# A block kernel's sixth norm takes the early form, and every head rounds its fourth weight tile ahead of its first evacuation

## What is computed

```python
h = rms_norm(x, gain) * (1.0 + scale) + shift      # the norm ahead of a sublayer
y = h @ w_first                                    # its first projection, in 128-column tiles
...
x = x + (1.0 + gate) * out                         # the residual behind it
```

## Time and profile before

| | |
|---|---|
| median of 3 runs | 3580.46 us (3576.4 to 3591.96) |
| the profiled execution | 3580.06 us, its span 3578.2 us |
| PE busy, share of span | 3448.2 us, 96% |
| DVE, ACT, POOL busy | 2018.7 us (56%), 1212.7 us (34%), 360.7 us (10%) |
| granted PE clock, mean | 0.983 |
| w_hi (L246), w_lo (L252) | 475 and 480 of them, mean 1097 and 1321 ns |

### The profile page before, as it was taken

One profiled execution on the slowest core, in us unless ns is written; L12 is line 12 of the kernel. 1 busy time (PEld: TensorE's weight loads), 2 busy tenths in 40 slices (PEclk: granted clock), 3 DMA queues, 4 the chain that ended last, 5 costly groups with the idle time before them and its releaser, 6 DMA issues. The chain is left out here.

```text
span 3578.2 us, 56582 instructions
## 1 busy us (share of the span) xinstructions
PE 3448.2 (96%) x22456; PEld 2780.9 (78%) x22456; DVE 2018.7 (56%) x2820; ACT 1212.7 (34%) x1783; POOL 360.7 (10%) x264
## 2 busy tenths in 40 slices
PE   7999999999999999999999999999988999999998
PEld 5888777878888788876678888877757787878886
DVE  6666666846665666575443433365666773464343
ACT  3222346432222322243343322233434543233231
POOL 1000003410000000000101000130103330010000
PEclk9999999999999999999999999999979999989999
DMA  6554321125553455421032222222210002223232
GB/s 246 197 193 169 125 76 71 55 93 188 188 207 139 179 191 203 156 86 54 1 112 88 96 97 106 84 88 83 63 33 6 8 6 73 95 65 100 89 99 71
DMA packets 103765, 382.75 MB, mean 107 GB/s; under 512 B 11424, under 2 KB 15136, under 8 KB 103200
## 3 DMA queue, kind: packets, MB, share of 16 engines
q1 hardware_dynamic: 103584, 380.15, 30.7%
HBM read 378.01 MB, written 2.10 MB: 106 GB/s over the span
## 5 line engine op out<-in xcount | busy, mean ns | idle before, releaser
L457 PE MATMUL bank<-h_hi,w_hi 128*128 128x512 f32 x2576 | 1015.5, 394 | 29.2 <-DVE w_lo L252 26.5
L459 PE MATMUL bank<-h_hi,w_lo 128*128 128x512 f32 x2576 | 1005.6, 390 | 0.0
L458 PE MATMUL bank<-h_lo,w_hi 128*128 128x512 f32 x2576 | 1005.3, 390 | 0.0
L252 DVE TENSOR_TENSOR w_lo<-w_raw,w_hi 128x1024 fp32r<-128x1024 f32 (+2 forms) x480 | 634.3, 1321 | 397.7 <-ACT w_hi L246 386.5
L246 ACT ACTIVATE w_hi<-w_raw 128x1024 fp32r<-128x1024 f32 (+2 forms) x475 | 521.1, 1097 | 299.8 <-PE bank L459 260.4
L457 PEld LDWEIGHTS bank<-h_hi,w_hi 128*128 128x128 f32 x2576 | 485.3, 188 | 146.5 <-DVE w_lo L252 30.0
L459 PEld LDWEIGHTS bank<-h_hi,w_lo 128*128 128x128 f32 x2576 | 485.0, 188 | 102.4
L458 PEld LDWEIGHTS bank<-h_lo,w_hi 128*128 128x128 f32 x2576 | 485.5, 188 | 100.7 <-issue 1.9
L457 PE MATMUL bank<-f_gu_hi,w_hi 128*128 128x512 f32 x704 | 278.5, 396 | 0.0
L458 PE MATMUL bank<-f_gu_lo,w_hi 128*128 128x512 f32 x704 | 278.2, 395 | 0.0
L459 PE MATMUL bank<-f_gu_hi,w_lo 128*128 128x512 f32 x704 | 278.2, 395 | 0.0
(11 more groups left out here) (645 smaller groups left out, 4759.4 us busy)
## 6 DMA issues: line engine op xcount, KB each, us to landing
ada_tiles<-in_ada SPq DMA_DIRECT2D x180, 512.0 KB, 4.3
w_raw<-in_gu SPq DMA_DIRECT2D x176, 512.0 KB, 4.4
w_raw<-in_dn SPq DMA_DIRECT2D x64, 704.0 KB, 5.0
w_raw<-in_w_ff SPq DMA_DIRECT2D x64, 512.0 KB, 3.5
w_raw<-in_w_hyb SPq DMA_DIRECT2D x36, 512.0 KB, 3.4
w_raw<-in_w_rkv SPq DMA_DIRECT2D x24, 512.0 KB, 3.5
w_raw<-in_w_attn SPq DMA_DIRECT2D x20, 512.0 KB, 3.5
w_raw<-in_w_hout SPq DMA_DIRECT2D x16, 512.0 KB, 3.4
```

Of the source, the lines that this page charges most:

```text
L252: K.nc.vector.tensor_tensor(K.w_lo[:, half, 0:kb * P], K.w_raw[:, slot, 0:kb * P], K.w_hi[:, half, 0:kb * P].bitcast(F32), ALU.subtract).t ...
L457: nc.tensor.matmul(K.ps[bank][:], wh, hi, start=start, stop=False)
L458: nc.tensor.matmul(K.ps[bank][:], wh, lo, start=False, stop=False)
L459: last_mm = nc.tensor.matmul(K.ps[bank][:], wl, hi, start=False, stop=stop)
```

## The change

1. `hybrid` is given `follow`, the `Modulated` of f01, which is now built with early=True. Its out projection makes the gain at its start and splits x times gain after each residual, on ACT behind the square and on DVE behind the residual. The parts go to `hyb_ahead_hi` and `hyb_ahead_lo`, in the chunks of `proj` from `GATE` and from `Z`. `early_tile` reads them there; in the other heads `ahead_hi` and `ahead_lo` are h_hi and h_lo as before.
2. In every early head the weights of tile 3 are rounded (ACT) and subtracted (DVE) at t == 0, ahead of evacuation 0, instead of at t == 1 behind it. What they wait for is as before.

```diff
@@ gemm, ACT and DVE bodies @@
                     if head and isinstance(i, int) and t < 3:
-                        if t < 2 and not (early and t == 0):
+                        if early and t == 0:
+                            split_hi(K, act, kb, 3 % RING, 1, g0 + 3)
+                        elif t < 2 and not early:
                             split_hi(K, act, kb, (t + 2) % RING, t % SPLIT, g0 + t + 2)
...
                     if head and isinstance(i, int) and t < 3:
-                        if t < 2 and not (early and t == 0):
+                        if early and t == 0:
+                            split_lo(K, dve, kb, 3 % RING, 1, g0 + 3)
+                        elif t < 2 and not early:
                             split_lo(K, dve, kb, (t + 2) % RING, t % SPLIT, g0 + t + 2)
@@ early_tile @@
-                    hi, lo, bank, start, stop = mm(c, 0)
+                    _, _, bank, start, stop = mm(c, 0)
+                    hi, lo = head.ahead_hi[:, c, :], head.ahead_lo[:, c, :]
@@ class Modulated @@
         self.gain, self.scale, self.shift, self.early = gain, scale, shift, early
+        self.ahead_hi, self.ahead_lo = K.h_hi, K.h_lo
...
     def ahead_act(self, act, o):
         K = self.K
-        K.nc.scalar.activation(K.h_hi[:, bass.ds(o, 1), :], K.x[:, bass.ds(o, 1), :], ACT.Identity, scale=K.gain[:, bass.ds(o, 1)]).then_inc(K.h_hi_done.sem, 1)
+        K.nc.scalar.activation(self.ahead_hi[:, bass.ds(o, 1), :], K.x[:, bass.ds(o, 1), :], ACT.Identity, scale=K.gain[:, bass.ds(o, 1)]).then_inc(K.h_hi_done.sem, 1)
...
@@ hybrid @@
-def hybrid(K, nxt, head, gate):
+def hybrid(K, nxt, head, gate, follow):
...
     squares = Squares(K, "hyb", A + 2 * DC * CH)
+    follow.ahead_hi = K.at("hyb_ahead_hi", [P, DC, S], F32R, A + GATE * CH)
+    follow.ahead_lo = K.at("hyb_ahead_lo", [P, DC, S], F32R, A + Z * CH)
...
             act.wait_ge(free.sem, free(o + 1))
+            act.wait_ge(K.x_written.sem, K.x_written(follow.GAIN_STEPS))
             squares.by_act(act, K.x[:, o:o + 1, :], o, o % 2)
+            follow.ahead_act(act, o)
...
             v.scalar_tensor_tensor(x, K.ps[HOUT_BANK[o]][:], K.coef[:, o:o + 1], x, ALU.mult, ALU.add).then_inc(free.sem, 1)
+            follow.ahead_dve(dve, o)
...
         dve.wait_ge(K.coef_done.sem, K.coef_done(1))
+        follow.gain_ahead(dve)
...
+    follow.ahead_advance()
     free.base += DC
@@ build @@
-            elif step != "hyb":
+            else:
                 follow = Modulated(K, *terms(K, *places[plan[n + 1]]), early=True)
...
-                    hybrid(K, nxt, head, gate)
+                    hybrid(K, nxt, head, gate, follow)
```

More of the change, by code:

```diff
@@ L720, in ahead_dve @@
         dve.wait_ge(K.h_hi_done.sem, K.h_hi_done(o + 1))
-        K.nc.vector.scalar_tensor_tensor(K.h_lo[:, bass.ds(o, 1), :], K.x[:, bass.ds(o, 1), :], K.gain[:, bass.ds(o, 1)],
-                                         K.h_hi[:, bass.ds(o, 1), :].bitcast(F32), ALU.mult, ALU.subtract).then_inc(K.h_ready.sem, 1)
+        K.nc.vector.scalar_tensor_tensor(self.ahead_lo[:, bass.ds(o, 1), :], K.x[:, bass.ds(o, 1), :], K.gain[:, bass.ds(o, 1)],
+                                         self.ahead_hi[:, bass.ds(o, 1), :].bitcast(F32), ALU.mult, ALU.subtract).then_inc(K.h_ready.sem, 1)
     def ahead_advance(self):
```

## The result

The changed kernel takes 3602.59 us (median of 8 runs, 3594.4 to 3613.21), the kernel before 3584.1 us (8 runs, 3576.4 to 3593.84). The ratio is 1.0047 with the interval 1.0033 to 1.006: 16.8 us slower (11.8 to 21.5). It is not the quotient of the two medians, which lie 18.5 us apart. The forecast was 15.0 us slower, 3595.1 us when counted from the one execution that the prediction started from (3580.06 us); the kernel before measures 4.0 us more than that here.

The account below looks back on a forecast made before the run. PE was taken to bound the kernel, busy 96% of the span. Terms of -2.25 (early f01 head), +12.0 (DVE queue) and +5.3 (clock) gave +15.0 us, 3595.1 us from 3580.06; recorded range 3577 to 3602 us.

Parts of the forecast that it names:

- Part A: f01's head made early, with its parts made in the hybrid's out projection: 2.25 us gained, throttled stretch included.
- Idle DVE: In hyb, ml, f10, f01 and b2, DVE would stand idle about 1.9 us before tile 3's `w_lo`.
- hyb 1.91, ml 1.94: In these two heads tile 4 would start later by 1.91 us (hyb) and 1.94 us (ml).
- f10 3.08: In f10's head the second modulation transfer is issued later, so tile 4 starts 3.08 us later; bounds 1.3 to 4.1.
- f01 3.08: f01's new early head has the same DVE queue as f10's, so tile 4 again starts 3.08 us later.
- b2 1.98: In b2's head, DVE's delayed queue would cost 1.98 us ahead of tile 4.
- The clock: Long PE idle gaps ahead of tile 4 lower its clock: 1.05 us for each of five heads, 5.3 us in all.
- the one priced gap: The 4.49 us of PE idle before 543.12, whose following tile took 7.71 us against 5.7: a 2.0 us price.
- the second rival: Full clock price after every long gap ahead of tile 4: 10 us of clock, +19.8 us, 3599.8 us; chance 0.20.
- f11 nothing: In f11's head DVE has nothing to do before tile 3, so the reordering would lose nothing.
- gain at tile 3 kept: Rival: tile 4's wait is set by something that doesn't move, so the pull pays: -6.7 us, 3573.4 us; chance 0.14.
- The out projection kept its cover: Rounding ahead costs nothing there, 0.8 us of cover staying; the rival, cover lost, adds 3 us, 3598.1 us; chance 0.04.

Follow-up runs that it names:

- e1: The changed kernel with tile 3's weights put back behind evacuation 0, leaving only f01's early head; 3584.47 us, ratio 0.9988 to the kernel before.
- e2: The kernel before with only tile 3's weights moved ahead of evacuation 0, f01 keeping the old head; 3599.64 us, ratio 1.0033.
- e7: The changed kernel with only DVE's new order, ACT's edit undone; a single run, 3599.22 us.
- e9: The changed kernel with throwaway matmuls between tiles 3 and 4, 20 in f01 and f10, 16 in hyb, ml and b2; 3599.62 us, ratio 1.0037.
- e5: The changed kernel with tile 4's weights also rounded and subtracted ahead of evacuation 2; 3585.27 us, ratio 0.9994 to the kernel before.
- e3: The changed kernel with throwaway matmuls between tiles 3 and 4, 20 in f01 and f10, 8 in hyb, ml and b2; 3600.84 us, ratio 1.0041.
- e8: e4 with tile 3's subtraction ahead of the last modulation step or convolution tap of evacuation 0 (not b2, f11); 3570.66 us, ratio 0.9958 to before.
- e6: The changed kernel with only ACT's new order, DVE's edit undone; a single run, 3586.3 us.
- e4: e1 with tile 4's weights rounded and subtracted ahead of evacuation 2 instead of behind it; 3577.83 us, ratio 0.9964 to the kernel before.

## Why the prediction was right

The order of the argument held: e1, e2 and e7 put the loss on DVE's part of the reordering, e9 puts the rest on the clock. The median itself, 3602.59 us, lies above the recorded range of 3577 to 3602, because that range was counted from 3580.06 us and the kernel before measured 3584.1 beside it; what was forecast is the difference. The interval of the ratio (1.0033 to 1.006) reaches over the half percent that the prediction gave as its line, so these runs do not settle on which side of that line the change lies. The single terms:

- **Part A, -2.25.** Right in kind, too large: e1's head takes 30.62 us where I had 30.02 (30.32 - 0.3). In the same kernel f10's head takes 30.90 instead of 30.32, without being touched, and the old form of f01's head takes 31.22 us in e2 instead of 32.27, so one head read once was sure to about 1 us, and the term can be anything from 0.6 to 1.65. The form itself brings tile 3 forward by 3.0 us (23.09 in e1 against 26.05), but tile 4 then waits 1.80 us instead of 0.62. That the rounding ahead costs nothing in the out projection held: in e1 DVE has 0.88 us of idle time ahead of a residual there where I had worked out 0.8.
- **Idle DVE, 1.91 to 1.98.** 1.86 us in hyb, f01, f10 and ml, 1.95 in b2, as derived from the places of `w_hi` and DVE's first work.
- **hyb 1.91, ml 1.94.** Measured 1.94 and 1.94.
- **f10 3.08.** The later issue is exact; the term was mis-sized by the transfer, 6.63 us instead of 5.17, beyond my bound of a microsecond more. 4.54 was measured here, 3.9 in e7 (34.21 - 30.32) and 2.8 in e2 (33.10 - 30.32): the transfer's time is not constant, and 3.08 lies among them. The trace of before already held a longer one than the row I took and bounded from, f01's of 6.22 us, so the bound was too narrow by a row that I had not read. What lengthens the transfer was not tried.
- **f01 3.08.** 33.28 - 30.62 = 2.66; its transfer was waited for 5.46 us.
- **b2 1.98.** Mis-sized: 0.85. DVE's idle time is there (1.95 us), but I took each DVE operation behind it to last as before, and from the first L2624 to `w_lo` of tile 4, `w_lo` of tile 3 left out, they take 1.2 us less: the second L2637 took 0.68 us, the same instruction 1.78 before. The earlier trace rows begin a stretch in which POOL works beside DVE in both kernels; that the lengths depend on how the two meet is my reading, and no run isolates it. DVE's timeline of before, then of after:

```profile
2362.13 1.78 DVE L2624 TENSOR_TENSOR lora<-shift_raw 128x512 f32<-128x512 f32 x1
```
```profile
2394.60 0.68 DVE L2637 TENSOR_TENSOR lora<-shift_raw 128x512 f32<-128x512 f32 x1
```

- **The clock, 1.05 for each of five.** Mis-sized: 1.6 in hyb and ml, 2.3 and 2.5 in f10 and f01, nothing in b2, 8.0 against 5.3. Half the price of the one priced gap was a choice between two ends; the second rival's full price (10) is nearer to four of the five heads. And that one price was itself a draw. The idle 4.5 us ahead of hyb's second projection stand in all eleven profiles, and from its first to its 24th matmul a tile behind them took between 6.79 us (the changed kernel) and 8.09 (e5), 7.48 in before, where a tile at the full clock takes 5.35. The Trainium skill's statement (TensorE: Matmul & The Clock Gate, "What's actually happening") that the gate's window runs freely, from which the prediction took that a gap's place decides its price, agrees with that spread, and with the short gaps: 2.09 us ahead of b2's tile 4 cost nothing and 2.09 in e3's ml 1.6 us. But its lower end, nothing, did not occur for long ones: each of the 24 gaps of 3.9 us and more ahead of a tile of 24 such matmuls in these profiles was paid for, with 1.4 us or more.
- **f11 nothing.** 27.85 against 27.83.

The parts came to 10.3 us where I had 9.75 (12.0 - 2.25), b2's shortfall hiding f10's excess, and to 8.0 of clock where I had 5.3. The sum of 15.0 was near 16.8 partly because errors of both signs met, and that is luck. Of the rivals, "gain at tile 3 kept" is refuted by tile 4's later start in all five heads (f01's against e1's); its core returns in e8, and even there most of the gain is lost two tiles later. The out projection kept its cover.

## What to carry to other kernels

When an instruction is pulled forward on an in-order engine, ask not when its consumer needs it but when its own input is there: the time in which the engine stands in front of it is debt for the work behind, and is collected at the next place without slack (tile 4 here, tile 5 in e5 and e8; f11, which has slack, paid nothing). Pull the item that the consumer waits for and whose input has long been there (tile 4's weights: 6.6 us, about 0.2%, faster than e1), not the one whose input arrives last. And price a PE gap with the matmuls behind it: in the four heads that lost clock, it took another 0.36 to 0.47 of the idle time.

## What the runs showed that I had not expected

**A short gap can be enough for the lower clock.** Besides e3's hyb and ml (2.15 and 2.09 us of idle time), the f01 head of e6 has 2.02 us of idle time ahead of tile 4 and then runs it at 0.76, and the changed kernel loses clock behind the 1.60 us ahead of 558.05. The b2 head of the changed kernel has 2.09 and keeps 1.00; e1's f01 head has 1.80 and keeps it; and 2.74 us ahead of 3024.93 in the changed kernel are followed by 24 matmuls at 1.00, where the same gap in before (2.73, ahead of 2994.68) is followed by 0.76. Between 1.6 and 2.8 us the length of a gap does not say what comes. The windows over tile 3 of hyb (behind 4.00 us of idle time) and tile 4 of f01 (behind 2.02) in e6 show the same 0.76 behind both:

```profile
438.18:445.40 7.22, 7.22 (x25) 5.78 (x26) 6.51 (x9) 0.64 (x1) 0.00 (x0) 0.76 0.24 73
827.27:834.44 7.17, 7.17 (x24) 5.77 (x25) 6.08 (x9) 1.57 (x2) 0.00 (x0) 0.76 0.44 151
```

**The mLSTM's own matrices lose clock in one execution and keep it in another.** In a stretch of the mLSTM stage behind its first projections, which the change does not touch, the profile of after has three windows of 17 us at 0.80, 34 us apart, in step with the stage's repetition:

```profile
1725.00:1742.00 17.00, 17.00 (x58) 11.06 (x59) 5.53 (x15) 4.05 (x6) 3.04 (x3) 0.80 0.00 0
1742.00:1759.00 17.00, 16.22 (x86) 11.64 (x84) 8.80 (x20) 6.46 (x18) 2.46 (x5) 1.00 0.00 1
1759.00:1776.00 17.00, 17.00 (x58) 11.07 (x59) 5.52 (x15) 3.98 (x6) 2.97 (x3) 0.80 0.00 0
1776.00:1793.00 17.00, 16.27 (x85) 11.63 (x84) 8.80 (x20) 6.53 (x18) 2.54 (x5) 1.00 0.00 1
1793.00:1810.00 17.00, 16.83 (x74) 12.35 (x75) 4.13 (x10) 2.39 (x4) 0.00 (x0) 0.80 0.00 1
```

The stretch from one DVE subtraction of weights to another, the same pair in each kernel, takes 164.8 us in the profile of before, 164.7 in e1, 166.5 in e3, 166.9 in e8, but 174.5 in the changed kernel and in e9, 176.2 in e2 and 171.9 in e4. In e7 it is 164.4, in e5 165.3 and in e6 166.8. e2, e3, e5, e7 and e9 all have DVE's new order and fall on both sides, and e4, without it, is among the long ones. So it goes with the single execution and not with the edit, as far as one profile of each can show. From shortest to longest it is 12 us, beside a spread of 17 between the eight runs of before (3576.4 to 3593.84 us). It accounts for 9.7 us of the 32 between the two profiled spans. Whether the change makes the slow outcome more likely by where it moves this stretch in time was not tried.
